# Experts' row sum, final norm and next model's first norm as one block by token tile

## The reference, cut to what matters

```python
# end of the first model
h = h + sum over the two chosen experts c of gates[:, c] * y[:, c]      # moe_swiglu
x = rms_norm(h, final_norm_g)                                           # first_block's result
# start of the second model
mod = silu(c_2) @ w_ada_2 + b_ada_2        # shift1, scale1, ...
h2 = rms_norm(x, g_mix_2) * (1 + scale1) + shift1
proj = h2 @ w_in_2                          # 1024 x 2496
```

## Time and profile before

| | us |
|---|---|
| median of 3 runs (lowest, highest) | 4557.43 (4549.16, 4559.23) |
| the profiled execution, its own time | 4559.06 |
| span of the profiled execution, first to last instruction | 4557.0 |
| experts' last store issued | 2719.07 |
| first gather of `combine_stage` starts on GpSimd | 2723.26 |
| first matmul of the projection | 2777.57 |

### The profile page before, as it was taken

How to read it: one execution, slowest core, us unless ns; L and a number is a source line. 1 busy time by engine, 2 the same in 40 slices (tenths; PEclk the granted TensorE clock), 3 DMA queues, 4 the chain that set the end, 5 groups by cost and what they waited for, 6 DMA issues and landing times. The chain is left out here.

```text
span 4557.0 us, 45375 instructions
## 1 busy us (share of the span) xinstructions
PE 3855.7 (85%) x17173; PEld 2566.8 (56%) x17180; DVE 1715.8 (38%) x3657; ACT 585.3 (13%) x1486; POOL 1099.9 (24%) x1165
## 2 busy tenths in 40 slices
PE   7988999999676999999999986998666777676666
PEld 3465777644645888888999983465322223222222
DVE  2042231111941000000000004184988776777655
ACT  1121000112320000000000001143111111111111
POOL 0010000000411000000000000000477777777775
PEclk9969999999897999999999998979788888888888
DMA  3103674320017888888777752102799999999998
GB/s 117 56 2 132 235 264 162 138 74 19 1 56 286 298 301 303 307 304 298 257 260 249 259 197 67 54 1 80 298 406 404 420 417 412 420 416 415 418 415 337
DMA packets 531782, 1088.29 MB, mean 239 GB/s; under 512 B 36993, under 2 KB 315934, under 8 KB 531526
## 3 DMA queue, kind: packets, MB, share of 16 engines
q1 hardware_dynamic: 376330, 522.81, 33.5%
q0 software_dynamic: 150976, 546.79, 29.8%
q10 hardware_dynamic: 4348, 17.07, 0.9%
HBM read 1065.29 MB, written 21.28 MB: 238 GB/s over the span
## 5 line engine op out<-in xcount | busy, mean ns | idle before, releaser
L2634 PE MATMUL banks<-peer_ring,mix 128*128 128x512 f32 x1512 | 843.2, 718 | 359.6 <-DMA peer_ring<-in_peer_v_dram,peer_expert 359.6
L2634 PEld LDWEIGHTS banks<-peer_ring,mix 128*128 128x128 f32 x1512 | 337.8, 231 | 861.3 <-DMA peer_ring<-in_peer_v_dram,peer_expert 452.2
L2902 DVE SCALAR_TENSOR_TENSOR peer_ring<-peer_ring,banks 128x1024 f32<-128x1024 f32 x512 | 593.6, 1217 | 250.1 <-DMA peer_ring<-in_peer_u_dram,peer_expert 249.1
L2502 POOL DMA_INDIRECT peer_ring<-in_peer_u_dram,peer_expert x512 | 481.3, 940 | 658.8 <-DVE peer_expert L2836 456.2
L2502 POOL DMA_INDIRECT peer_ring<-in_peer_v_dram,peer_expert x512 | 488.1, 953 | 162.1 <-issue 143.7
L1809 DVE TENSOR_TENSOR experts_hid<-experts_gs,banks 128x128 f32<-128x128 f32 (+1 forms) x224 | 66.5, 297 | 1169.4 <-ACT experts_gs L1781 1169.4
L1690 PEld LDWEIGHTS banks<-rows_xt,experts_wg 128*128 128x128 f32 x3584 | 447.6, 192 | 36.9 <-issue 36.6
L1690 PE MATMUL banks<-rows_xt,experts_wg 128*128 128x128 f32 (+1 forms) x3584 | 463.1, 283 | 3.2 <-DVE rows_xt L1629 3.2
L1690 PE MATMUL banks<-rows_xt,experts_wu 128*128 128x128 f32 (+1 forms) x3584 | 461.8, 282 | 0.0
L1690 PEld LDWEIGHTS banks<-rows_xt,experts_wu 128*128 128x128 f32 x3584 | 441.8, 192 | 0.0
L402 PE MATMUL banks<-xT,proj_w 128*128 128x512 f32 (+2 forms) x736 | 328.1, 604 | 8.7 <-PEq L216 7.1
(11 more groups left out here) (449 smaller groups left out, 3635.1 us busy)
## 6 DMA issues: line engine op xcount, KB each, us to landing
experts_wg<-in_moe_w_gate_dram SPq DMA_DIRECT2D x112, 1024.0 KB, 5.1
experts_wu<-in_moe_w_up_dram SPq DMA_DIRECT2D x112, 1024.0 KB, 7.7
experts_wd<-in_moe_w_down_dram SPq DMA_DIRECT2D x112, 1024.0 KB, 8.1
ada_w<-in_w_ada_dram SPq DMA_DIRECT2D x12, 2048.0 KB, 8.0
ffn_wg<-in_ffn_w_gate_dram SPq DMA_DIRECT2D x22, 1024.0 KB, 7.9
ffn_wu<-in_ffn_w_up_dram SPq DMA_DIRECT2D x22, 1024.0 KB, 10.4
ffn_wd<-in_ffn_w_down_dram SPq DMA_DIRECT2D x22, 1024.0 KB, 11.9
proj_w<-in_c_w_in_dram SPq DMA_DIRECT2D x8, 2048.0 KB, 8.5
```

Source lines behind the costliest of these rows:

```text
L2502: pool.indirect_dma_start(out=ring[:, slot_of(kind, n, b), :], out_offset=None, in_=tables[kind == "value"], in_offset=bass.IndirectOffset ...
L2634: last = nc.tensor.matmul(ps[bank + hf][:, :], diag[:, n % 2 * B + b, :], ring[:, slot_of("value", n, b), hf * 512:(hf + 1) * 512], start= ...
L2902: nc.vector.scalar_tensor_tensor(row, row, 1.0, rows_at, ALU.mult, ALU.mult, accum_out=acts[:, t % 2, at:at + 1]).then_inc(dotted[q].sem, 1)
```

## The change

`combine_stage`, the call of `row_norm_stage` for "final1" and the call of `norm_stage` for "norm4" are replaced by one block, `second_norm_stage`. Four things differ:

- Each token tile has its own arrival semaphore. The steps of a tile (sum of the rows, square, inverse, root, gain, square, inverse, root, scale, transpose, place) are issued in a software pipeline: iteration `n` works on tile `n`'s sum, tile `n-1`'s first inverse, tile `n-2`'s gain, and so on.
- SyncE starts the final gain and then all of `ahead` at the start of this block, so beside the gathers.
- The gathered rows go into the buffers `qb`, `kb`, `vb`, `va`, and the final gain into `ka`, which the second model fills only later.
- The shift is added together with the gain while a bank is placed into `xT`: per tile four ScalarE instructions (first bank) and four VectorE instructions (second bank) of 128x128, instead of two VectorE instructions of 128x512 and the one addition over all of `xT`.

The small routing tensors (`gates`, `row_of`) now live until the second model's end.

```diff
-def combine_stage(S, R):
...
-                dve.wait_ge(got.sem, got.at(16 * 2 * TT))
-                for c in range(2):
-                    for t in range(TT):
-                        nc.vector.scalar_tensor_tensor(S.h[:, t, :], yg[:, t, c, :], R.gates[:, t, c:c + 1],
-                                                              S.h[:, t, :], ALU.mult, ALU.add).then_inc(own.sem, o.up())
-                    dve.wait_ge(own.sem, o.value())
+def second_norm_stage(S, R, M, rows, final_gain, xn, ahead):
...
+        def place(eng, t, half, op):
+            eng.wait_ge(turned.sem, turned.at(2 * t + half + 1))
+            for kk in range(4):
+                k = 4 * half + kk
+                op(xT[:, k, t * P:(t + 1) * P], ps[2 * t + half][:, kk * P:(kk + 1) * P], M.gain1[:, k:k + 1], M.col[:, k:k + 1])
...
+            @block.sync
+            def _(sp):
+                sp.dma_start(final_gain, S.a["final_norm_g"].partition_broadcast(P)).then_inc(got.sem, 16)
+                ahead(sp)
...
+                for t in range(TT):
+                    for c in range(2):
+                        pool.indirect_dma_start(out=rows[t][:, c, :], out_offset=None, in_=R.y,
+                                                in_offset=bass.IndirectOffsetOnAxis(ap=R.row[:, t, c:c + 1], axis=0),
+                                                ).then_inc(arrived[t].sem, 16)
...
+                def join(t):
+                    dve.wait_ge(arrived[t].sem, arrived[t].at(32))
+                    for c in range(2):
+                        if c:
+                            dve.wait_ge(joined.sem, joined.at(2 * t + 1))
+                        nc.vector.scalar_tensor_tensor(h[:, t, :], rows[t][:, c, :], R.gates[:, t, c:c + 1], h[:, t, :], ALU.mult,
+                                                       ALU.add).then_inc(joined.sem, 1)
...
+                for n in range(TT + 5):
+                    if 0 <= n - 5 < TT:
+                        place(dve, n - 5, 1, shifted)
+                    if 0 <= n - 3 < TT:
+                        invert(ss[:, n - 3, 1:2], n - 3, n_squares, n_own, n_inverse)
+                    if 0 <= n - 2 < TT:
+                        scale(n - 2)
+                    if 0 <= n - 1 < TT:
+                        invert(ss[:, n - 1, 0:1], n - 1, squares, own, inverse)
+                    if n < TT:
+                        join(n)
...
+                for n in range(TT + 4):
+                    if 0 <= n - 3 < TT:
+                        root(n - 3, 1, n_inverse, n_roots)
+                        normalise(n - 3)
+                    if 0 <= n - 2 < TT:
+                        act.wait_ge(ready.sem, ready.at(n - 1))
+                        square(n - 2, 1, n_squares)
+                    if 0 <= n - 1 < TT:
+                        root(n - 1, 0, inverse, roots)
+                    if n < TT:
+                        act.wait_ge(joined.sem, joined.at(2 * n + 2))
+                        square(n, 0, squares)
+                    if 0 <= n - 4 < TT:
+                        place(act, n - 4, 0, shifted)
...
-                norm_stage(S, "norm4", M.gain1[:, :], shift=M.col[:, 0:KD], ahead=ahead, xn=mix)
+                rows = [x[:, :, :].rearrange("p a b -> p (a b)").rearrange("p (c d) -> p c d", c=2) for x in (A.qb, A.kb, A.v, A.va)]
+                final_gain = A.ka[:, 0:2, :].rearrange("p a b -> p (a b)")
+                second_norm_stage(S, R, M, rows, final_gain, mix, ahead)
...
-    moe1(S, xn_rows)
-    row_norm_stage(S, "final1", S.a["final_norm_g"])
     with ExitStack() as st:
+        R = Routing()
+        moe1(S, R, xn_rows, st)
```

More of the change, by code:

```diff
@@ L1863, in expert_values @@
     return eng.value_load(tile, min_val=lo, max_val=hi)
-def moe1(S, xn_rows):
-    nc, a = S.nc, S.a
-    with ExitStack() as st:
[L1870 to L1880, removed]
@@ L1884, in combine_stage, with moe1 @@
-def combine_stage(S, R):
[L1885 to L1889, removed]
+def moe1(S, R, xn_rows, st):
+    nc = S.nc
+    R.gates = S.sb("gates", [P, TT, 2], F32, st)
+    R.row = S.sb("row_of", [P, TT, 2], I32, st)
+    R.expert = S.sb("expert_of", [P, 2, 16], I32, st)
+    R.units = S.sb("n_units", [P, 2], I32, st)
+    R.xn = xn_rows
+    R.y = nc.dram_tensor("y_rows", (ROWS_MAX, D), F32, kind="Internal").ap()
+    R.token_of_row = nc.dram_tensor("token_of_row", (LISTED, 1), I32, kind="Internal").ap()
+    route_stage(S, R)
+    experts_stage(S, R)
@@ new lines, in second_norm_stage @@
+def second_norm_stage(S, R, M, rows, final_gain, xn, ahead):
+    nc, h, xT, ps = S.nc, S.h, S.xT, S.ps
+    ident = S.const("ident")
+    arrived = [S.sig(f"y_arrived{t}", pool_dma=True) for t in range(TT)]
+    joined = S.sig("c_own")
+    got, squares, own, inverse, roots, ready = (S.sig("w_" + x) for x in ("got", "squares", "own", "inverse", "roots", "ready"))
+    n_squares, n_own, n_inverse, n_roots, normed, turned = (
+        S.sig("n_" + x) for x in ("squares", "own", "inverse", "roots", "normed", "turned"))
+    with ExitStack() as st:
+        ss = S.sb("second_ss", [P, TT, 2], F32, st)
+        r = S.sb("second_r", [P, TT, 2], F32, st)
+        def place(eng, t, half, op):
[3 more added lines that the diff above has]
+                op(xT[:, k, t * P:(t + 1) * P], ps[2 * t + half][:, kk * P:(kk + 1) * P], M.gain1[:, k:k + 1], M.col[:, k:k + 1])
+        with nc.Block("second_norm") as block:
+            @block.sync
+            def _(sp):
+                sp.dma_start(final_gain, S.a["final_norm_g"].partition_broadcast(P)).then_inc(got.sem, 16)
+                ahead(sp)
@@ L1893, in _ @@
                     for c in range(2):
-                        pool.indirect_dma_start(out=yg[:, t, c, :], out_offset=None, in_=R.y,
+                        pool.indirect_dma_start(out=rows[t][:, c, :], out_offset=None, in_=R.y,
                                                 in_offset=bass.IndirectOffsetOnAxis(ap=R.row[:, t, c:c + 1], axis=0),
-                                                ).then_inc(got.sem, 16)
+                                                ).then_inc(arrived[t].sem, 16)
@@ L1907, in combine_stage @@
-        got.base += 32 * TT
-        own.base += 8
+                def join(t):
[5 more added lines that the diff above has]
+                                                       ALU.add).then_inc(joined.sem, 1)
@@ new lines, in invert, with scale @@
+                def invert(x, t, done, mine, out):
+                    dve.wait_ge(done.sem, done.at(t + 1))
+                    nc.vector.tensor_scalar(x, x, 1.0 / D, EPS, ALU.mult, ALU.add).then_inc(mine.sem, 1)
+                    dve.wait_ge(mine.sem, mine.at(t + 1))
+                    nc.vector.reciprocal(x, x).then_inc(out.sem, 1)
+                def scale(t):
+                    dve.wait_ge(roots.sem, roots.at(t + 1))
+                    if t == 0:
+                        dve.wait_ge(got.sem, got.at(16))
+                    nc.vector.scalar_tensor_tensor(h[:, t, :], h[:, t, :], r[:, t, 0:1], final_gain, ALU.mult,
+                                                   ALU.mult).then_inc(ready.sem, 1)
@@ new lines, in shifted @@
+                def shifted(dst, src, gain, shift):
+                    nc.vector.tensor_scalar(dst, src, gain, shift, ALU.mult, ALU.add)
+                for n in range(TT + 5):
[9 more added lines that the diff above has]
+                        join(n)
@@ new lines, in _, with square, root, normalise @@
+            @block.scalar
+            def _(act):
+                def square(t, i, done):
+                    nc.scalar.activation(xn[:, t, :], h[:, t, :], ACT.Square, accum_out=ss[:, t, i:i + 1]).then_inc(done.sem, 1)
+                def root(t, i, before, done):
+                    act.wait_ge(before.sem, before.at(t + 1))
+                    nc.scalar.activation(r[:, t, i:i + 1], ss[:, t, i:i + 1], ACT.Sqrt).then_inc(done.sem, 1)
+                def normalise(t):
+                    act.wait_ge(n_roots.sem, n_roots.at(t + 1))
+                    nc.scalar.activation(xn[:, t, :], h[:, t, :], ACT.Copy, scale=r[:, t, 1:2]).then_inc(normed.sem, 1)
+                def shifted(dst, src, gain, shift):
+                    nc.scalar.activation(dst, src, ACT.Identity, scale=gain, bias=shift)
+                for n in range(TT + 4):
[12 more added lines that the diff above has]
+                        place(act, n - 4, 0, shifted)
@@ new lines, in _ @@
+            @block.tensor
+            def _(pe):
+                for t in range(TT):
+                    pe.wait_ge(normed.sem, normed.at(t + 1))
+                    for half in range(2):
+                        for kk in range(4):
+                            k = 4 * half + kk
+                            last = nc.tensor.transpose(ps[2 * t + half][:, kk * P:(kk + 1) * P], xn[:, t, k * P:(k + 1) * P], ident)
+                        last.then_inc(turned.sem, 1)
```

(12 more changed lines are left out.)

1 line of the change is left out of this document (removed).

## The result

| | before, us | after, us |
|---|---|---|
| median (lowest, highest) of 22 runs each | 4558.19 (4547.39, 4566.81) | 4573.49 (4560.03, 4582.55) |
| the profiled execution, its own time | 4559.06 | 4570.06 |
| its span | 4557.0 | 4568.4 |

The ratio is 1.0033, with a 95% interval of 1.0025 to 1.0041: the kernel became **slower by some 15 us**. Forecast were 16 us in the other direction, with a chance of 3% for slower.

What follows compares the result with a forecast made beforehand. The 53.98 us from the first gather to the projection were taken as all on the path. 8.5 + 29.6 = 38.1 us there, 15.9 less, gave 4557.43 - 15.9 = 4541.5 us, range 4534 to 4551.

Steps and rivals of the forecast that it cites:

- Whatever these 53.98 us become moves everything behind them: First gather to VectorE's last instruction before the projection took 53.98 us; any saving there was to shift everything later equally.
- The wait for all gathers goes; later tiles are not waited for: In the block, only tile 0's gathers are waited for; tiles land at 8.5, 12.3, 16.1 and 19.9 us.
- two-thirds share: Gathers' share of the transfers beside the weights: a gather takes 1.9 us, a tile 3.8.
- a0: Time from the block's first gather until tile 0's two gathers have landed: 8.5 us, between 7.4 and 9.6.
- the two-to-one of the earlier trace: Gathers beside weight chunks of chunk 0's form kept 65.1% against 31.8%, landing in 7.1 us.
- The chain behind a0 = 29.6 us: VectorE to the last sum 15.66, ScalarE to the last scaled tile 10.79, last transposes and placing 3.14 us.
- the bounds were 1.1 and 1.4: VectorE's four placings of the second bank into `xT` take 1.1 to 1.4 us; 1.1 was taken.
- The block = 38.1 us: First gather to the block's end: 8.5 + 29.6 = 38.1 us against 53.98, 15.9 us less.
- SyncE's loads end before the block: Transfers are over at about 30 us after the first gather; the wait for `b_forget` lies 8 us before the block's end.
- The clock costed at nothing: TensorE's clock at the projection's start got no cost; 2 us gained or lost were allowed.
- the rival for "slower": Projection held longer at 1.2 GHz: 32 us more eat the gain, 50 us more make it 0.2% slower; chance 3%.
- If the stretch shrinks by 16 us and the kernel does not: Stated sign of a wrong prediction: the block gets 16 us shorter but the whole kernel does not.

Runs made afterwards that it cites:

- ring_by_224: Kernel before with 224 unused bytes ahead of `peer_ring` and 32 behind, so only the ring leaves its 256-byte boundary: 4588.30 us, ratio 1.0074.
- block_and_pad_32: Changed kernel with an unused tile of 32 bytes per partition ahead of `mix`, putting `peer_ring` back on a multiple of 256: 4545.84 us, ratio 0.9977.
- block_ring_realigned: Changed kernel with 32 unused bytes ahead of `peer_ring` and 224 behind, so the ring alone is back on a multiple of 256: 4548.28 us, ratio 0.9982.
- block_late_loads: block_and_pad_32 with SyncE's `ahead` held back until the last tile's gathers have landed; the final gain still loads beside them: 4540.56 us, ratio 0.9970.
- late_loads_all_aligned: Changed kernel with `ahead` held back until the gathers landed, and `mix`, the gathered rows' buffers and `peer_ring` on multiples of 256 bytes: 4538.07 us, ratio 0.9961.
- block_all_aligned: Changed kernel, loads early as it has them, with the same padding as late_loads_all_aligned: 4540.39 us, ratio 0.9963.

## Why the prediction was wrong

**The step that failed** is not in the sum of the block. It is "Whatever these 53.98 us become moves everything behind them", by which nothing behind the block was to change but its start. The change's last point, that the small routing tensors "now live until the second model's end", got no term in the sum and no rival. Their 224 bytes move the ring of the last stage off its 256-byte boundary. That costs 29 us there (shown both ways: ring_by_224 adds it without the block, block_and_pad_32 and block_ring_realigned take it away with the block). The profile of the kernel before could have priced the risk, though not told of it: 1024 gathers run in a stage whose DMA engines are full, so any per cent there is 13 us, nearly as much as the block had to give.

Point by point:

- *The wait for all gathers goes; later tiles are not waited for.* Right: the only wait for gathers is tile 0's. The reason given for the later tiles came true partly by luck. The prediction took 1.26 us of work for a gather, while its own 11.9 / 8 gives 1.5; at a two-thirds share the tiles would then have landed at 13.0, 17.6 and 22.1 us, each after VectorE was to ask (12.7, 17.0, 21.6). In the run the last gather landed after some 21.1 us (issued at 2731.21, 12.4 us to landing at most), and VectorE, itself late by the 2.3 us of tile 0, asked for that tile at 23.2.
- *a0 = 8.5 us, range 7.4 to 9.6.* Mis-sized: 2733.30 - 2722.48 = 10.8, outside the range. With only the final gain beside it a0 is 7.4 (block_late_loads), the lower bound, so the weights' part is 3.1 to 3.4 us and not 1.1 (a0 is 10.5 in block_and_pad_32). The shares suggest why: I took the two-to-one of the earlier trace rows for the gathers, and they got 44.1% against 51.8%. With the Trainium skill's rule for the queues ("DMA: Bandwidth & Descriptors", Queues, rings and completion order) the sum would have been 0.4 to 1.7 us longer: the right sign, and still too small.
- *The chain behind a0 = 29.6 us.* Measured 28.4: the last sum ends 14.98 us after the first began (15.66 in the sum), the last tile is scaled 9.96 us later (10.79), the last placing ends 3.43 us after that (3.14). VectorE's pieces run closer together than their durations: the gain of tile 0 starts at 2739.91, 0.09 us before the sum ahead of it, 2737.40 + 2.60, is over. The placing in the form that no row had, gain and shift on VectorE, took 1.35 to 1.37 us for four; the bounds were 1.1 and 1.4 and I had taken the wrong end.
- *The block = 38.1 us.* Measured 39.2 to VectorE's last instruction, since a0's 2.3 us too many and the chain's 1.2 too few cancel in part: the gain is 14.8 us in place of 15.9 at the first matmul.
- *SyncE's loads end before the block.* Right: `b_forget` is issued at 2746.10, 16 us before the barrier. The weights' issues took 18.58 us in place of 8.18, and nothing waited for them.
- *The clock costed at nothing.* Wrong by 3.9 us in the projection. The sum looked for it at the projection's start, where only 0.6 us of it is; the rest comes 70 us in and later. It was also the rival for "slower", at 3% and with a far larger price than it has; by itself it leaves the kernel 10.9 us faster. The 3% came true in sign, by a cause that the prediction did not have.
- *"If the stretch shrinks by 16 us and the kernel does not"* the prediction was to be wrong. That is what came.

With the ring on its boundary the edit gives what the block and the projection add up to: -14.8 + 3.9 = -10.9 us, 4545.84 against 4556.75. The version to keep is late_loads_all_aligned, 4538.07 us against 4556.66, below both kernels; its interval overlaps those of block_late_loads (4540.56) and block_all_aligned (4540.39), so that it is the best of the three is not shown.

## What to carry to other kernels

A change that keeps even a few bytes allocated for longer moves every buffer behind them, so compare the start of the large buffers before and after, and where a stage is bound by gathers into one of them, try its start on a multiple of 256 bytes; the padding cost nothing here. For the eight gathers of this block the runs are too coarse to show a price. When a local change moves the total the wrong way, cut both traces at events that both have and make a table of the stages before forming a theory: here it pointed 400 us past the edit at once. And where transfers already set the length of a stage, price each risk to them by the whole stage.

## What was not expected of the hardware

- 4 KB rows gathered into SBUF at 32, 64, 128 or 224 bytes past a multiple of 256 moved at 405 to 406 GB/s in place of 415, over 2% less, and landed in 6.7 to 6.9 us (median) in place of 6.2. The stage's length was the same for every distance, 1378.6 to 1379.4 us.
- Eight gathers started in the same 10 us as the projection's chunks landed after 8.8 to 12.4 us, where the earlier trace rows had 4.3 to 6.4 without them.
- The granted clock in one stage (0.66 for 0.78, 0.88 for 1.00) differed with what had run some 80 us earlier, in seven of eight profiles. Neither 14 us more of rest nor the addresses by themselves changed it.
